# Rolling the middle iterations of the MLP stage of a hybrid decoder layer into hardware loops

## What is computed

```python
x = x + merged @ w_out                                   # stage "out"
hm = jnp.square(jax.nn.relu(rmsnorm(x, norm_mlp) @ w_up))  # w_up: 2048 x 8192
x = x + hm @ w_down                                      # w_down: 8192 x 2048
y = rmsnorm(x, norm_final)
```

## Time and profile before

| | |
|---|---|
| median of 3 executions | 2227.45 us (2224.47 to 2227.63) |
| the profiled execution | 2224.47 us |
| its span, first to last instruction | 2222.6 us |
| TensorE busy | 2161.2 us (97%) |
| VectorE / ScalarE busy | 1226.5 / 780.5 us |
| granted TensorE clock, mean | 0.995 |
| MLP stage on TensorE | from 1300.0 to 2203.3 us |

### The profile page before, as it was taken

One profiled execution on the slowest core, in us unless ns is written; L12 is line 12 of the kernel. 1 busy time (PEld: TensorE's weight loads), 2 busy tenths in 40 slices (PEclk: granted clock), 3 DMA queues, 4 the chain that ended last, 5 costly groups with the idle time before them and its releaser, 6 DMA issues.

```text
span 2222.6 us, 36091 instructions
## 1 busy us (share of the span) xinstructions
PE 2161.2 (97%) x14489; PEld 2093.4 (94%) x14489; DVE 1226.5 (55%) x1988; ACT 780.5 (35%) x938; POOL 156.0 (7%) x318
## 2 busy tenths in 40 slices
PE   6999998999999999999999999999999999999997
PEld 5999898899998899989999999999999999999996
DVE  5877677555557555555545454444444444444444
ACT  5334555222223222233333433333333333333342
POOL 3000002101023100010000100000000000000001
PEclk9999999999999999999999999999999999999998
DMA  5444344333454333436444444444454445444442
GB/s 166 142 151 150 111 137 146 91 101 115 124 160 135 97 116 102 124 106 200 151 152 151 151 136 158 150 148 148 152 152 151 145 151 150 154 143 153 150 143 95
DMA packets 294448, 308.84 MB, mean 139 GB/s; under 512 B 9584, under 2 KB 290288, under 8 KB 294080
## 3 DMA queue, kind: packets, MB, share of 16 engines
q1 hardware_dynamic: 290464, 291.54, 42.0%
q0 software_dynamic: 3584, 15.55, 2.4%
q10 hardware_dynamic: 288, 0.15, 0.0%
HBM read 298.83 MB, written 8.37 MB: 138 GB/s over the span
## 4 chain that ended last, share of the span: by engine, by line
PE 87%; DVE 7%; ACT 3%; issue 2%; DMA 0%; DVEq 0%; ACTq 0%; SPq 0%
PE main L1319 26%; PE main L1321 26%; PE main L1320 26%; PE aux L1415 6%; ACT hi L557 2%; DVE scratch L802 2%; DVE lo L802 1%; DVE scratch L809 1%; PE aux L1398 0%; DVE scratch L805 0%; PE aux L1388 0%; DVE scratch L806 0%; DMA raw<-in_w_in 0%; DVE merged L809 0%; PE aux L1519 0%
## 5 line engine op out<-in xcount | busy, mean ns | idle before, releaser
L802 DVE TENSOR_TENSOR lo<-raw,hi 128x1024 fp32r<-128x1024 f32 x546 | 670.5, 1236 | 571.2 <-ACT hi L557 565.2
L557 ACT ACTIVATE hi<-raw 128x1024 fp32r<-128x1024 f32 x546 | 573.1, 1056 | 930.7 <-PE main L1321 923.0
L1319 PE MATMUL main<-x_hi,hi 128*128 128x320 f32 x2688 | 842.2, 313 | 5.6 <-DVE lo L802 5.6
L1320 PE MATMUL main<-x_lo,hi 128*128 128x320 f32 x2688 | 831.5, 309 | 0.0
L1321 PE MATMUL main<-x_hi,lo 128*128 128x320 f32 x2688 | 831.4, 309 | 0.0
L1319 PEld LDWEIGHTS main<-x_hi,hi 128*128 128x128 f32 x2688 | 505.7, 188 | 13.4 <-issue 6.7
L1320 PEld LDWEIGHTS main<-x_lo,hi 128*128 128x128 f32 x2688 | 505.8, 188 | 0.6
L1321 PEld LDWEIGHTS main<-x_hi,lo 128*128 128x128 f32 x2688 | 505.4, 188 | 0.0
L1319 PE MATMUL main<-o_hi,hi 128*128 128x320 f32 x1408 | 442.4, 314 | 4.6 <-DVE o_lo L802 4.6
L1321 PE MATMUL main<-o_hi,lo 128*128 128x320 f32 x1408 | 435.6, 309 | 0.0
L1320 PE MATMUL main<-o_lo,hi 128*128 128x320 f32 x1408 | 435.6, 309 | 0.0
(11 more groups left out here) (225 smaller groups left out, 1171.6 us busy)
## 6 DMA issues: line engine op xcount, KB each, us to landing
raw<-in_w_in SPq DMA_DIRECT2D x210, 512.0 KB, 3.6
raw<-in_w_up SPq DMA_DIRECT2D x128, 512.0 KB, 3.7
raw<-in_w_down SPq DMA_DIRECT2D x128, 512.0 KB, 3.4
raw<-in_w_back SPq DMA_DIRECT2D x80, 512.0 KB, 3.4
scratch<-in_s_in POOLq DMA_DIRECT2D x8, 512.0 KB, 4.7
out_s_out<-scratch POOLq DMA_DIRECT2D x8, 512.0 KB, 4.6
merged<-in_x SPq DMA_DIRECT2D x4, 640.0 KB, 9.2
qkv<-in_x POOLq DMA_DIRECT2D x1, 2560.0 KB, 10.6
```

Of the source, the lines that this page charges most:

```text
L557: act.activation(HI[:, slot * TILE:(slot + 1) * TILE], RAW[:, slot * TILE:(slot + 1) * TILE], ACT.Copy).then_inc(hi_ready, 1)
L802: return dve.tensor_tensor(out, a, b, op)
L1319: pe.matmul(bank, hi, xh, start=first, stop=False)
L1320: pe.matmul(bank, hi, xl, start=False, stop=False)
```

## The change

The MLP stage's iterations become loops on the engines: on SyncE all eight, on the three compute engines iterations 1 to 6, while 0 and 7 stay written out. The work and its order within each engine stay the same. The targets of waits in the loops are worked out in registers, and the rows of `w_down` and columns of `w_up` are addressed from a register. TensorE and VectorE had written out iterations 1 to 7 alike; iteration 7 now stands behind the loop.

```diff
-            for it in range(8):
+            with sp.Fori(0, 8) as it:
                 for j in range(16):
                     load(MLP_N, 32, it, j, A["w_up"], j % 4 * 512, it * 1024 + j // 4 * 256)
...
             mlp(0, {4: [lambda: residual(7)], 6: [lambda: root(4)]})
-            for it in range(1, 7):
+            with act.Fori(1, 7) as it:
+                ch.enter(it, 1, LINKS["mlp"])
                 mlp(it, {})
+                ch.leave(6, "mlp")
             mlp(7, {down_tile(d) + 4: [lambda d=d: last_squares(d)] for d in range(6)})
...
             mlp(0, {4: [lambda: residual(3, 1)], 6: [rms_mlp]})
-            for it in range(1, 8):
-                mlp(it, {2: [lambda it=it: down(it - 1, 6)], 3: [lambda it=it: down(it - 1, 7)]})
+            with dve.Fori(1, 7) as it:
+                mlp(it, {2: [lambda: down(it - 1, 6)], 3: [lambda: down(it - 1, 7)]})
+            mlp(7, {2: [lambda: down(6, 6)], 3: [lambda: down(6, 7)]})
...
             mlp(0, {3: [(7, lambda: sum_squares(8))]})
-            for it in range(1, 8):
+            with pe.Fori(1, 7) as it:
                 mlp(it, {})
+            mlp(7, {})
             sum_squares(16)

-LINKS = {"qkv": 6, "lru": 8, "gpl": 4, "gpp": 6, "rglru": 1}
+LINKS = {"qkv": 6, "lru": 8, "gpl": 4, "gpp": 6, "rglru": 1, "mlp": 4}
```

## The result

The changed kernel takes 2257.85 us (median of 4, 2255.88 to 2259.87) against 2227.43 us for the kernel before: a ratio of 1.0145, with a 95% interval of 1.0131 to 1.0160. (The ratios here come from the single executions and are not exactly those of the medians, which would be 1.0137.) It is slower by 30.4 us, and the time lies outside the predicted range.

The account below looks back on a forecast made before the run. The prediction took TensorE's matmul rate to bound the MLP stage. Register work, branches, helpers, strip 3 and fetching (if the body is held) each added 0 to the median of 2227.45 us, giving 2227.5 us, range 2223.5 to 2235.

Parts of the forecast that it names:

- The bound: MLP stage: bound by TensorE's rate at the full 2.4 GHz, 112.64 us per iteration, with no time to give back.
- Register work, helpers, SyncE: MLP loops: register work on TensorE, ScalarE's and VectorE's loops, and SyncE's loads each cost 0.
- The branch and its cover: TensorE's back edges: a 0.21 us branch hidden by 2.3 us of queued work, cost 0; uncovered, five cost 1 us.
- The tightest hand-over: TensorE's tile 18 waiting for strip 3's remainder: 1.1 us of room, chain ending 0.4 us later in a loop, cost 0.
- Fetching instructions: TensorE's back edges over a body of 6.2 packets: cost 0 if the body is held, left open by the trace.
- rival A: TensorE's back edges: body not held, each waits for a fetch, 1.1 us per edge, 2233 us (2228.5 to 2255.5); chance 0.21.
- Rivals B and C: B: strip 3's hand-over makes TensorE wait, 2230.5 us, chance 0.03. C: less fetching speeds the stage, 2225.3 us, chance 0.04.
- Slower by over 0.2%: Whole kernel: chance 0.13 of a measured slowdown above 4.5 us, 0.11 of it from rival A.

Follow-up runs that it names:

- all_but_pe: The changed kernel with TensorE's iterations 1 to 6 written out again, SyncE, ScalarE and VectorE still rolled; 2226.00 us, ratio 1.0002.
- shift16: The changed kernel with 16 semaphore increments that nobody waits for at the start of TensorE's program; 2224.92 us, ratio 0.9995.
- short_bodies: The changed kernel with TensorE's iterations 1 to 7 written out, each with two short loops inside, 28 back edges in all; 2226.80 us, ratio 1.0001.
- spread192: The changed kernel with 192 unused semaphore increments on TensorE, 6 behind each tile of the written-out iteration 0; 2225.65 us, ratio 1.0003.
- shift222: The changed kernel with 222 unused semaphore increments at the start of TensorE's program; 2260.34 us, ratio 1.0164.
- spread224: The changed kernel with 224 unused semaphore increments on TensorE, 7 behind each tile of the written-out iteration 0; 2236.69 us, ratio 1.0052.

## Why the prediction was wrong

**The bound.** Right: TensorE's rate bounds the stage, and whatever stops TensorE shows in full.

**Register work, helpers, SyncE.** Right at 0, shown for the other engines by `all_but_pe` with its turns of 675.84 us, and for TensorE by `shift16`, in which all of the change's register work is there, and by `short_bodies`.

**The branch and its cover.** Right: 0.21 us, hidden by 2.3 us of queued work, wherever the target is held (`shift16`, `spread192`, `short_bodies`).

**The tightest hand-over.** Right that it has room. In `shift16` the remainder of strip 3 ends 5.64 us behind the end of that strip's last matmul, 5.62 before; the loops add 0.02 us, not the 0.4 allowed for.

**Fetching instructions: the step that failed.** The sum took 0 "if the body is held", and 0.72 as the chance of no change, though the rows left a jump back over 6.2 packets open. Measured were 6.8 us per edge, 33.8 in all. What counts isn't the length alone but how many packets the body touches. 1,596 instructions touch seven or eight, by where they start, and with an eighth touched the first is gone at the back edge. That rival A's mechanism is what happened is shown by the branches, the packets and the shifts. That the store is eight packets, of which one is fetched ahead as a packet is entered, is the simplest reading of the limit between 1,778 and 1,810, and of 54 packets with no refetch; the runs don't look into the store. The q8 packets of `shift16` fit it: seven start in the first turn (1411.3 to 1519.0 us), none in the other five, and the next at 2101.9, 14.7 us behind the last branch. At 1,596 instructions in 112.64 us, the 190 that are left in the seventh packet behind that branch take 13.4 us; so the eighth packet had been kept since the first turn, unexecuted, and entering it set off the next fetch. That reading agrees with the 2,048 instructions that the Trainium skill (Runtime: NRT & Kernel Launch, "Instruction fetch mechanics") gives for TensorE, and against that section's other rule, of two lines, `shift16` jumps back over seven packets in 0.21 us. (The prediction says that by this rule every loop here would stall. That goes too far: the out loop's turn of 192 matmuls and as many loads is only some 1.6 packets.)

The trace of before gives a hint of the place, which the prediction didn't look for. Its q8 packets in two pieces, 1411.5 to 1413.5 us (none) and 1413.5 to 1413.6:

```profile
q1 hardware_dynamic: 499, 0.50, 77.6%
...
q8 instruction: 1, 0.02, 62.6%
```

TensorE's sequencer, 2.5 us ahead, began iteration 1 at 1414.8 - 2.5 = 1412.3 us. In the changed kernel the second packet starts 0.67 us behind the end of the branch at the first back edge (1526.42 + 4.27 = 1530.69, packet at 1531.36), and 0.8 to 1.3 us behind it at the others. So here a new packet was entered between 1412.3 and 1412.9 us, 0 to 0.6 us or none to eight instructions behind the start of the iteration, at 14 instructions per us. This is an estimate from two traces, in hindsight. It says that the body starts within some ten instructions of a packet's border, and leans to the side ahead of it, the worst place that was run; but just behind the border is a place where `shift16` lost nothing, and the reading is too coarse to rule that out.

**The price of rival A.** Taken as 1.1 us per edge, measured 6.8, above the upper end of 3.9 + 1.7 = 5.6. The duration of the fetch was in bounds: 4.27 us of branch less the cover gives a stall of 2.0. What was missing is the second stall, 2.35 us at the first edge and 2.7 in the mean: the term priced one fetch per edge, and with ten instructions left in the first packet there are two, one behind the other. The halved clock was named, but only for the upper end of the range and behind a single idle time of 3.4 us. Here it came at all five edges, 0.9 to 1.7 us behind a first stall of 1.6 to 2.0 us and before the second stall was over, and it cost 2.2 us and not 1.7. Which part of the two stalls brings it isn't shown: in `shift222` one stall of 2.0 us was enough at one edge, and four of 1.9 to 2.1 us were not.

That less than 3.4 us can be enough stood in the trace of before, outside the rows that the prediction read: an idle time of 2.15 us, and the stretch that begins 0.7 us behind it.

```profile
387.61 0.61 PE L1441 MATMUL aux<-ident,scratch 128*128 128x128 f32 x3 [2.15 <-DVE scratch L802]
...
388.32:391.74 3.42, 3.42 (x14) 3.08 (x15) 0.94 (x4) 0.13 (x1) 0.00 (x0) 0.50 0.02 5
```

**Rivals B and C.** Neither showed: no wait at tile 18, iteration 0 unchanged at 114.79 us.

**The chances.** "Slower by over 0.2%" had 0.13. The rows gave no reason to hold a body of 6.2 packets for safe: the longest shown to be held was 3.5.

## What to carry to other kernels

Before a long loop is rolled on TensorE, count the 256-instruction packets that its body touches, not its length: up to seven were free here, and an eighth cost 2.4 to 6.8 us at each back edge. Sixteen idle instructions ahead of the loop were enough to get all of 30 us back; the shorter inner loops of `short_bodies` did the same, and bodies that short touch three packets at most wherever they lie. On an engine that bounds a stage, compare the duration of its loop branches in the profile: 0.2 us is a hit, 4 us is a miss.

## What the runs showed of the hardware

- A back edge of TensorE to code no longer held kept its sequencer for 3.6 to 4.8 us, against 0.21 us to code that is held. After such a miss nothing of the body was reused: nine packets were fetched in every turn of the changed kernel behind a back edge.
- TensorE's clock fell to 0.50 at all five edges of the changed kernel, for 6.83 us each: behind an idle time of 1.6 to 2.0 us and three matmuls, and before the end of a second one of 2.35 to 3.3 us. In `shift222`, where an idle time of 1.9 to 2.1 us was followed by one of 0.4 us at most, it stayed at 1.00 but for one edge of five, where it fell 1.15 us after the matmuls had started again, for 3.41 us.
- Semaphore increments by TensorE's sequencer at the program's start delayed the first matmul by 0.16 us each (32 more of them, 5.07 us); 7 behind each tile of 24 matmuls in `spread224` didn't delay it (iteration 0 at 114.76 us).
